# Second layer's latents taken from the un-normalised stream: a change to a two-block transformer kernel

## The chip, the cores and the metric

The kernel runs on one core of one Trainium2 chip. The metric is the device time of one execution in microseconds (us), of which the span from the first to the last instruction of the profile is nearly all.

## The reference, cut to what matters

A first block (two attention layers) is followed by a second block of two like layers. Each layer of the second block computes this on a stream `x` of 512 tokens by 1024 features in fp32:

```python
for l in range(2):
    h = rmsnorm(x, pre_norm_g[l])              # x * rsqrt(mean(x*x) + eps) * g
    proj = h @ w_in[l]
    (u, v, z_a, c_q, c_kv, k_rope, z_b, x_c, z_c, g_a, g_b, g_c) = jnp.split(proj, cuts, axis=-1)
    y_a = gmlp_spatial(u, v, ...) * silu(z_a)
    y_b = mla_attention(c_q, c_kv, k_rope, ...) * silu(z_b)
    y_c = rg_lru(x_c, ...) * silu(z_c)
    merged = sigmoid(g_a)*(y_a @ w_a) + sigmoid(g_b)*(y_b @ w_b) + sigmoid(g_c)*(y_c @ w_c)
    x = x + rmsnorm(merged @ w_out[l], post_norm_g[l])
```

`mla_attention` begins with `rmsnorm(c_q)` (384 wide, 3 tiles of 128) and `rmsnorm(c_kv)` (256 wide, 2 tiles); these five tiles are "the latents". `k_rope` is rotated by position and not normalised.

## The kernel before, in words

Features lie on the 128 partitions, the 512 tokens along the free axis, so `x` is 8 tiles of 128 x 512. A product in near-fp32 is three matmuls: every weight and every activation is split into an upper part (rounded) and a lower part (the rest), and upper*upper, upper*lower and lower*upper are added up in one bank (`products`, L553). One output tile of a 1024-wide input is thus 8 x 3 = 24 matmuls.

Weights come as a stream of slots of 128 x 1024 in an order written out by hand (`layer_stream`): in each layer of the second block ckv0, ckv1, cq0, cq1, cq2, kr, zb0, zb1, uv0, uv1, up0 and so on. SyncE's queue loads a slot into one of two raw buffers as soon as the slot two places before it has been split; ScalarE rounds it into one of five ring places (L1220) when TensorE has given that place back; GpSimd subtracts to get the lower part in four pieces (L507). ScalarE issues its rounding inside its own fixed order of work (`feed`, called from `next_job`), so a slot is rounded only when ScalarE comes to that point of its program. All five engines run such written-out programs and wait on semaphores.

The place of the change is the turn from layer 0 to layer 1 of the second block. TensorE ends layer 0 with the eight jobs of `wo`; ScalarE copies each into `mixed` and squares it; the squares are added up over the partitions by a matmul with ones into the bank `stat`; ScalarE takes logarithm and exponential of the sum (`root`), and VectorE turns that into the inverse root by four operations (`inverse`, L1713 to L1719). VectorE then walks the eight tiles: scale `mixed` (L1724), add it to `x` (L2226). Behind it ScalarE squares each new tile of `x` (L1257), and TensorE adds up all eight squares by eight matmuls with ones. After the second root VectorE makes the inverse root of the pre-norm and walks the eight tiles again in `norm_in`: `h` = x * gain * inverse root, split into upper and lower, three operations a tile (L1724, L1728, L1729). TensorE runs a `group` of four latents at once, tile by tile as `h` comes, then cq2, the sum of the squares of ckv (`latent_sum`), kr, zb0, the sum of the squares of cq, the rotation of kr, zb1, uv0 and uv1, and then the first job of `up`. VectorE adds up the latents' squares (L2079), makes two inverse roots and splits five tiles into `y` (the `c` tiles, ckv first), from which uv and up read; `up` needs all of them.

At the start of layer 0 the kernel already works in the other way: ckv0 is projected tile by tile from `unscaled`, which is x * gain without the inverse root, and ckv1, cq and kr follow from it too. The latents are normalised afterwards anyway, so the missing factor cancels (the epsilon is put back by L2076); kr is multiplied by the inverse root on VectorE (L2088). There `h` is made by VectorE while TensorE runs these six jobs, and zb0 is the first job that reads `h`.

Of the kernel before, what the change touches and what calls it, by code (L numbers as in the profile page):

```python
# [25 lines left out]
P = 128  # L26
# [172 lines left out]
def build(nc, stream, x_in, mem_in, pos_in, const_in, tables_in, first_in, layer_in, rows_in, ws_in, out, plans):  # L199
# [312 lines left out]
    def pe_program(pe):  # L512
# [37 lines left out]
        def mm(o, lhsT, rhs, start, stop):  # L550
            return nc.tensor.matmul(o, lhsT, rhs, start=start, stop=stop)  # L551
# [86 lines left out]

        def group(S, C, W, slots, src, key, joins=(0, 0, 0, 0)):

            j0 = C.n["job"]
            ahead = [b for b in range(len(slots)) if joins[b] == 0]

            def term(b, k, w, v, start=False, stop=False):
                return mm(token_bank(j0 + b, b)[:, :], W.slot(slots[b])(k * P, k * P + P)[w], src[:, k, v, :], start, stop)

            for b in ahead:
                W.need(slots[b])  # L650
                if b == 0:
                    pe.wait_ge(*S.after(*(("h_upper", *key(0)[1:-1]) if key(0)[0] == "h" else key(0))))
# [44 lines left out]

        def added_squares(S, C, tag):
# [6 lines left out]
            mm(stat[:, :], c("ones"), std[:, (m + 1) % 2, :], True, False)  # L705
# [262 lines left out]
        for l in range(LAYERS):  # L968
# [3 lines left out]
            if l == 0:  # L972
                w = W.slot("ckv0")
                for k, _ in enumerate(job_units(S, C, W, [("ckv0", w(k * P, k * P + P), both(unscaled, k, 0, SEQ),
                                                           ("unscaled", k)) for k in range(KT)])):
                    if k == 3:
                        added_squares(first, C, "b")
                W.finish("ckv0")
                for name in ["ckv1"] + names("cq", QR) + ["kr"]:
                    full(S, C, W, name, unscaled, None)  # L980
                latent_sum("ckv", raw[:, 1, :])
            else:
                group(S, C, W, names("ckv", KVR) + names("cq", QR)[:2], h, hkey)
                full(S, C, W, "cq2", h, hkey)
                latent_sum("ckv", raw[:, 1, :])
# [206 lines left out]
            if l < LAYERS - 1:  # L1192
                squares(S, C, c("ones"), KT)
                continue
# [8 lines left out]
    def act_program(act):  # L1203
# [32 lines left out]

        def unscaled_upper(k):

            nc.scalar.activation(unscaled[:, k, 0, :], x[:, k, :], ACT.Copy, scale=lc(0, "pre", k))\
                .then_inc(*layers[0].mark("upper_rounded", ("unscaled_upper", k)))  # L1240

# [189 lines left out]
        for l, s in enumerate("ab"):  # L1431
# [73 lines left out]
            if s == "a":  # L1505
# [3 lines left out]
                    between=lambda i: memory_key(0) if s == "a" and i == 6 else None,  # L1509
                    behind=lambda i: unscaled_upper(i) if s == "b" else None)  # L1510
        act.dma_start(rot[:, :, :], tables_in).then_inc(cols_loaded, 16)

        for l in range(LAYERS):
# [16 lines left out]

            if l:
                root(S, C, 1.0 / (P * KVR), alone=True)
            if l:
                take_head()
            else:
                next_job(S, C)
                C.next("head")
            if l == 0:
                root(S, C, 1.0 / (P * KVR), alone=True, eps=False)
                take(S, C, b_gate(0), keys_=[("b_raw", 0)])  # L1540
            root(S, C, 1.0 / (P * QR), alone=True, eps=l > 0)
            if l == 0:
                loaded[0] = None
                act.wait_ge(*S.after("b_raw", 0))
                nc.scalar.activation(b_gate(0), b_gate(0), ACT.Silu).then_inc(*S.mark("taken", ("silu", "b", 0)))
            for t in range(1 if l == 0 else 0, 2):
                take(S, C, b_gate(t), ACT.Silu, keys_=[("silu", "b", t)])
            for g in range(2):
# [146 lines left out]
    def dve_program(dve):  # L1695
# [64 lines left out]

        def unscaled_lower(k):

            S = layers[0]
            dve.wait_ge(*S.after("unscaled_upper", k))
            link(S, nc.vector.scalar_tensor_tensor(out=unscaled[:, k, 1, :], in0=x[:, k, :], scalar=lc(0, "pre", k),
                                                   in1=unscaled[:, k, 0, :].bitcast(FP32), op0=ALU.mult, op1=ALU.subtract),
                 ("unscaled", k))
# [9 lines left out]

        def add_square(S, m, tag, i):

# [3 lines left out]
            dve.wait_ge(*S.after("sq", t))  # L1783
            acc = std[:, (m + 1) % 2, :]
            link(S, nc.vector.tensor_tensor(acc, sq[:, (t - 1) % 2, :] if i == 1 else acc, sq[:, t % 2, :], ALU.add),
# [169 lines left out]
        for l, s in enumerate("ab"):  # L1955
# [89 lines left out]
            for k in range(KT):  # L2045
# [12 lines left out]
                if s == "b" and k:  # L2058
                    unscaled_lower(k - 1)
        unscaled_lower(KT - 1)  # L2060
        inv = next_norm(S, C)

        for l in range(LAYERS):
            S = layers[l]
            norm_in(S, C, h, x, lambda k: lc(l, "pre", k), (), inv, own=l > 0)
            dve.wait_ge(cols_loaded, 16 * (l + 1))
            C.n["job"] += QR + KVR

            def add_latent(tag, acc, a, n):


                for i in range(l, n):
                    dve.wait_ge(*S.after("latent_sq", a + i))
# [4 lines left out]
                    else:  # L2078
                        link(S, nc.vector.tensor_tensor(acc, latent_sq[:, a, :] if l and i == 1 else acc,  # L2079
                                                        latent_sq[:, a + i, :], ALU.add), *done)  # L2080

# [3 lines left out]
            j = C.next("job")  # L2085
            if l == 0:
                dve.wait_ge(*S.after("job", j))
                link(S, nc.vector.tensor_tensor(nrm[:, n % 2, :], proj[j % 2][:, :], inv[1], ALU.mult),  # L2088
                     ("nrm", n), ("read", j), ("std_used", inv[0]))
            for name, a, tiles in (("ckv", QR, KVR), ("cq", 0, QR)):  # L2090
                m, sd = inverse(S, C, alone=1.0 / (P * tiles), eps=EPS if l else 0.0)
                for k in range(a, a + tiles):
# [324 lines left out]
```

## Time and profile before

| | |
|---|---|
| median of 3 runs | 2281.86 us (2278.32 to 2282.83) |
| the profiled execution | 2283.95 us, of which its span is 2282.1 us |
| mean granted TensorE clock | 0.987 of full speed |

A row of a timeline has the start in us, the duration in us, the engine, the line, the operation and the tiles; in square brackets the idle time before it and what ended that. PE is TensorE, DVE VectorE, ACT ScalarE, POOL GpSimd. Matmuls overlap, so their durations add up to more than the time that they take; starts are the better measure.

### The profile page before, as it was taken

What the parts mean: (1) busy time and instruction counts of PE and PEld (TensorE: products, weight loads), DVE (VectorE), ACT (ScalarE), POOL (GpSimd) and SP (SyncE); (2) the same over time, 40 slices, a digit from 0 to 9 for tenths busy, and PEclk for the clock granted to TensorE, in tenths of its full rate; (3) what the DMA queues carried; (4) which work ended last, traced back from release to release, by engine and by line L of the source; (5) the groups of instructions that cost most, each with busy time, mean ns of one, the idle gap of its engine ahead of it and who ended that gap; (6) DMA issues with size and microseconds to landing.
All of it is one profiled execution on the core that took longest, in us unless ns stands there. A gap on an engine that the chain in (4) does not pass through costs nothing.

```text
span 2282.1 us, 27440 instructions
## 1 busy us (share of the span) xinstructions
PE 2201.7 (96%) x10006; PEld 1695.3 (74%) x10006; DVE 1195.3 (52%) x1827; ACT 938.4 (41%) x1591; POOL 1157.0 (51%) x1360
## 2 busy tenths in 40 slices
PE   7999999999899999999999999799999999999998
PEld 5776567765587668888887788576678888877886
DVE  6877885558667341043248853564420342197642
ACT  4546643356444543232234622344532322237322
POOL 4553236642175224565466675263145665575852
PEclk9999999999999999999999999999999999999999
DMA  3222122321132113332233233122033332332321
GB/s 146 76 82 74 38 74 93 102 68 41 32 102 87 52 42 128 101 100 84 92 95 99 74 111 102 55 85 64 30 109 93 99 96 85 100 102 74 112 91 65
DMA packets 53127, 191.45 MB, mean 84 GB/s; under 512 B 6016, under 2 KB 6400, under 8 KB 52480
## 3 DMA queue, kind: packets, MB, share of 16 engines
q1 hardware_dynamic: 51696, 184.44, 25.7%
q10 hardware_dynamic: 1296, 5.24, 0.6%
q8 instruction: 81, 1.33, 0.2%
q14 instruction: 54, 0.44, 0.1%
HBM read 187.56 MB, written 2.10 MB: 83 GB/s over the span
## 4 chain that ended last, share of the span: by engine, by line
PE 80%; DVE 13%; ACT 3%; issue 2%; POOL 1%; DMA 1%; SPq 0%; DVEq 0%; ACTq 0%
PE proj L555 20%; PE proj L557 19%; PE proj L556 19%; PE score L551 4%; PE proj L551 3%; PE stat L551 2%; PE turned L551 2%; PE mix L551 2%; DVE small L1835 2%; PE score L555 2%; PE score L557 1%; PE score L556 1%; DVE tmp L1724 1%; PE ptp L802 1%; DVE prob L1824 1%
## 5 line engine op out<-in xcount | busy, mean ns | idle before, releaser
L507 POOL TENSOR_TENSOR lower<-raw_ring,upper 128x256 fp32r<-128x256 f32 x1340 | 1140.9, 884 | 1070.5 <-ACT upper L1220 1070.1
L555 PE MATMUL proj<-h,upper 128*128 128x512 f32 x1408 | 569.4, 404 | 9.3 <-DVE h L1729 2.7
L1220 ACT ACTIVATE upper<-raw_ring 128x1024 fp32r<-128x1024 f32 x335 | 351.6, 1060 | 543.4 <-PE proj L555 298.6
L557 PE MATMUL proj<-h,lower 128*128 128x512 f32 x1408 | 549.7, 390 | 0.0
L556 PE MATMUL proj<-h,upper 128*128 128x512 f32 x1408 | 549.1, 390 | 0.0
L555 PEld LDWEIGHTS proj<-h,upper 128*128 128x128 f32 x1408 | 265.0, 188 | 73.4 <-issue 5.9
L557 PEld LDWEIGHTS proj<-h,lower 128*128 128x128 f32 x1408 | 264.6, 188 | 56.4
L556 PEld LDWEIGHTS proj<-h,upper 128*128 128x128 f32 x1408 | 265.3, 188 | 50.4 <-issue 1.9
L555 PE MATMUL proj<-y,upper 128*128 128x512 f32 x586 | 234.8, 401 | 8.2 <-ACT qk L1324 5.7
L556 PE MATMUL proj<-y,upper 128*128 128x512 f32 x586 | 230.0, 393 | 0.0
L557 PE MATMUL proj<-y,lower 128*128 128x512 f32 x586 | 229.8, 392 | 0.0
L555 PEld LDWEIGHTS proj<-y,upper 128*128 128x128 f32 x586 | 111.1, 190 | 39.7 <-ACT qk L1324 7.1
L557 PEld LDWEIGHTS proj<-y,lower 128*128 128x128 f32 x586 | 111.1, 190 | 23.7
L556 PEld LDWEIGHTS proj<-y,upper 128*128 128x128 f32 x586 | 111.2, 190 | 22.9 <-issue 1.0
L2127 DVE TENSOR_TENSOR merged<-proj,gate 128x512 f32<-128x512 f32 x16 | 11.1, 692 | 154.2 <-PE proj L557 154.2
L1324 ACT ACTIVATE gate<-proj 128x512 f32<-128x512 f32 x48 | 28.8, 600 | 143.8 <-PE proj L557 143.8
L2130 DVE TENSOR_TENSOR tmp<-proj,gate 128x512 f32<-128x512 f32 x16 | 11.1, 692 | 140.3 <-PE proj L557 140.3
L802 PE MATMUL ptp<-const,prob 128*128 128x128 f32 x320 | 59.1, 281 | 9.5 <-DVE prob L1849 3.7
L1729 DVE TENSOR_TENSOR y<-tmp,y 128x512 fp32r<-128x512 f32 x62 | 64.1, 1033 | 2.1
L2182 DVE SCALAR_TENSOR_TENSOR tmp<-xpad,lcol,tmp 128x512 f32<-128x512 f32 x60 | 59.2, 986 | 2.1
L2160 DVE TENSOR_TENSOR tmp<-score,bs 128x512 f32<-128x512 f32 x16 | 11.1, 692 | 92.8 <-PE score L551 92.7
L1824 DVE TENSOR_TENSOR_SCAN prob<-prob 128x128 f32<-128x128 f32 (+3 forms) x48 | 44.5, 926 | 28.1 <-ACT prob L1348 26.7
(463 smaller groups left out, 3529.6 us busy)
## 6 DMA issues: line engine op xcount, KB each, us to landing
raw_ring<-stream SPq DMA_DIRECT2D x335, 512.0 KB, 3.5
landing<-stream SPq DMA_DIRECT2D x5, 512.0 KB, 9.3
x<-x_in SPq DMA_DIRECT2D x4, 512.0 KB, 6.0
rows<-rows_in ACTq DMA_DIRECT2D x2, 1024.0 KB, 5.3
out<-x SPq DMA_DIRECT2D x8, 256.0 KB, 2.4
memraw<-mem_in SPq DMA_DIRECT2D x1, 1024.0 KB, 12.6
memraw<-mem_in ACTq DMA_DIRECT2D x1, 1024.0 KB, 4.9
rot<-tables_in ACTq DMA_DIRECT2D x2, 512.0 KB, 4.0
```

Of the source, the lines that this page charges most:

```text
L507: ins = nc.gpsimd.tensor_tensor(lower[:, p % RING, a:b], slot_source(p)[:, a:b], upper[:, p % RING, a:b].bitcast(FP32), ALU.subtract)
L551: return nc.tensor.matmul(o, lhsT, rhs, start=start, stop=stop)
L555: first_ = nc.tensor.matmul(o, lhsT[0], rhs[0], start=start, stop=False)
L556: nc.tensor.matmul(o, lhsT[0], rhs[1], start=False, stop=False)
L557: return first_, nc.tensor.matmul(o, lhsT[1], rhs[0], start=False, stop=stop)
L802: ins = nc.tensor.transpose(bank_[:, kb * P:kb * P + P], src[:, kb * P:kb * P + P], c("ident"))
L1220: nc.scalar.activation(upper[:, p % RING, :], slot_source(p), ACT.Copy).then_inc(split_upper, 1)
L1324: nc.scalar.activation(dst, src[:, 0:cols], func, **more)\
L1729: link(S, nc.vector.tensor_tensor(dst[:, 1, :], src, dst[:, 0, :].bitcast(FP32), ALU.subtract), *keys_)
L1824: link(S, nc.vector.tensor_tensor_scan(rest[:, 0:n][:, ::-1], rest[:, 0:n][:, ::-1], rest[:, 0:n][:, ::-1], 1.0, ALU.mult, ALU.min))
L1835: link(S, nc.vector.reduce_max(small[:, 24 + b % 4:25 + b % 4], scores4[b % 4][:, 0:keys(kind, i)], AX_X))
L2182: link(S, nc.vector.scalar_tensor_tensor(out=dst, in0=src[:, k:k + SEQ], scalar=lc(l, "conv", LT * k + t), in1=dst, op0=ALU.mult, op1=ALU. ...
```

## The change

For layer 1 the kernel does what layer 0 does, with these differences: the update of `x` and the un-normalised split go together on VectorE (scale, add to `x`, add a square, lower part), four latents are projected at once (`group`), and the squares of `x` 0 to 5 are added up on VectorE into `raw[:, 1, :]`, so that TensorE adds three operands by ones in place of eight. That sum stands in TensorE's program in front of the group's last tile. ScalarE rounds the upper part (`unscaled_upper`) behind each square. The order after the group is that of layer 0: cq2, kr, sum of ckv, zb0, sum of cq. The diff, cut to its core:

```diff
-    unscaled = place("unscaled", at_y + 8 * 2 * SEQ, [P, KT, 2, SEQ], FP32R)
+    unscaled = [place(f"unscaled{l}", at, [P, KT, 2, SEQ], FP32R) for l, at in enumerate((at_y + 8 * 2 * SEQ, at_y + 13 * SEQ))]
...
             for k in range(1, KT):                       # in group(..., before_last=lambda: None)
+                if k == KT - 1:
+                    before_last()
                 pe.wait_ge(*S.after(*key(k)))
...
             else:                                        # TensorE, layer 1
-                group(S, C, W, names("ckv", KVR) + names("cq", QR)[:2], h, hkey)
-                full(S, C, W, "cq2", h, hkey)
-                latent_sum("ckv", raw[:, 1, :])
-                full(S, C, W, "kr", h, None)
-            full(S, C, W, "zb0", h, None if l else hkey)
+                group(S, C, W, names("ckv", KVR) + names("cq", QR)[:2], unscaled[1], lambda k: ("unscaled", k),
+                      before_last=lambda: added_squares(layers[0], C, "pre", raw[:, 1, :]))
+                for name in ("cq2", "kr"):
+                    full(S, C, W, name, unscaled[1], None)
+            latent_sum("ckv", raw[:, 1, :])
+            full(S, C, W, "zb0", h, hkey)
...
             added_squares(S, C, "wo")                    # TensorE, end of layer 0
             if l < LAYERS - 1:
-                squares(S, C, c("ones"), KT)
                 continue
...
             if l < LAYERS - 1:                           # ScalarE, end of layer 0
-                squares(S, C, [(x[:, k, :], ("x", k)) for k in range(KT)], 1.0 / DM)
+                plans["squares_at", (l, "pre")] = C.n["sq"]
+                squares(S, C, [(x[:, k, :], ("x", k)) for k in range(KT)], 1.0 / DM, behind=lambda i: unscaled_upper(1, i))
                 continue
...
                 step(S, nc.vector.tensor_tensor(x[:, d, :], x[:, d, :], mixed[:, d, :], ALU.add), ("x", d), ("std_used", m))
+                if l < LAYERS - 1 and d:                 # VectorE, end of layer 0
+                    add_square(S, m + 1, "pre", d - 1, raw[:, 1, :])
+                    unscaled_lower(1, d - 1)
             if l < LAYERS - 1:
+                unscaled_lower(1, KT - 1)
                 inv = next_norm(S, C)
```

`add_square` does something for tiles 1 to 5 alone. The rest of the diff makes the branches of layer 0 hold for both layers: the epsilon goes into VectorE's sum of the latents' squares (one operation more for each of ckv and cq), kr is scaled on VectorE, zb0's gate is copied first and put through Silu behind the second root.

## Rows read from the trace of the kernel before

**Rows 1.** The page: the chain that ended last, by engine.
```profile
PE 80%; DVE 13%; ACT 3%; issue 2%; POOL 1%; DMA 1%; SPq 0%; DVEq 0%; ACTq 0%
```

**Rows 2.** Stretches: PE, PEld, DVE, ACT, POOL busy; granted clock, DMA share, GB/s.
```profile
1452.00:1474.00 22.00, 10.73 (x16) 3.61 (x16) 17.74 (x25) 8.91 (x13) 0.00 (x0) 0.84 0.00 0
1474.00:1480.00 6.00, 5.80 (x19) 4.50 (x20) 5.76 (x8) 1.06 (x1) 3.80 (x4) 0.72 0.00 0
...
692.00:694.00 2.00, 0.61 (x3) 0.23 (x2) 1.93 (x3) 0.00 (x0) 1.11 (x1) 1.00 0.00 0
```

**Rows 3.** Timeline of all engines at the turn to layer 1.
```profile
1439.67 0.69 DVE L1785 TENSOR_TENSOR std<-std,sq 128x512 f32<-128x512 f32 x1 [4.75 <-ACT sq L1685]
...
1455.64 0.75 DVE L1724 SCALAR_TENSOR_TENSOR mixed<-mixed,lcol,std 128x512 f32<-128x512 f32 x1
...
1467.01 0.69 DVE L2226 TENSOR_TENSOR x<-x,mixed 128x512 f32<-128x512 f32 x1
...
1470.44 0.69 DVE L1713 TENSOR_SCALAR gate<-stat 128x512 f32<-128x512 f32 x1 [2.73 <-ACT std L1277]
...
1474.20 0.76 PE L551 MATMUL proj<-h,upper 128*128 128x512 f32 x1 [4.59 <-issue]
```

**Rows 4.** Timeline of VectorE in layer 1, from the normalised tiles on.
```profile
1473.34 0.75 DVE L1724 SCALAR_TENSOR_TENSOR h<-x,lcol,std 128x512 fp32r<-128x512 f32 x1
...
1490.35 0.69 DVE L1729 TENSOR_TENSOR h<-tmp,h 128x512 fp32r<-128x512 f32 x1
1499.00 0.96 DVE L2079 TENSOR_TENSOR raw<-latent_sq 128x512 f32<-128x512 f32 x1 [7.95 <-ACT latent_sq L1523]
...
1510.51 0.69 DVE L1713 TENSOR_SCALAR half_var<-stat 128x512 f32<-128x512 f32 x1
...
1532.67 1.11 DVE L1729 TENSOR_TENSOR y<-craw,y 128x512 fp32r<-128x512 f32 x1
```

**Rows 5.** Timeline of TensorE in layer 1: first matmuls of cq2, zb0 and up.
```profile
1497.70 0.39 PE L555 MATMUL proj<-h,upper 128*128 128x512 f32 x1
...
1509.62 0.50 PE L555 MATMUL proj<-h,upper 128*128 128x512 f32 x1
...
1533.83 0.50 PE L555 MATMUL proj<-y,upper 128*128 128x512 f32 x1 [0.31 <-DVE y L1729]
```

**Rows 6.** The chain that ended last, in order of time: six matmuls of the group.
```profile
1482.90 1.36 PE score L551 x6
```

**Rows 7.** Tile `unscaled`: operations, min/median/max ns, first and last start.
```profile
L1239 ACT ACTIVATE unscaled<-x,lcol x8: 709/711/717, 635.1 to 658.8; 128x512 fp32r<-128x512 f32 x8
L1765 DVE SCALAR_TENSOR_TENSOR unscaled<-x,lcol,unscaled x8: 754/1107/1112, 636.0 to 659.6; 128x512 fp32r<-128x512 f32 x8
```

**Rows 8.** Timeline of VectorE at the start of layer 0.
```profile
663.30 0.69 DVE L1713 TENSOR_SCALAR gate<-stat 128x512 f32<-128x512 f32 x1 [2.96 <-ACT std L1277]
...
666.21 0.75 DVE L1724 SCALAR_TENSOR_TENSOR h<-x,lcol,std 128x512 fp32r<-128x512 f32 x1
...
690.27 1.11 DVE L1729 TENSOR_TENSOR h<-tmp,h 128x512 fp32r<-128x512 f32 x1
...
692.56 1.09 DVE L2079 TENSOR_TENSOR raw<-raw,latent_sq 128x512 f32<-128x512 f32 x1
...
696.59 0.69 DVE L1713 TENSOR_SCALAR half_var<-stat 128x512 f32<-128x512 f32 x1
...
716.29 1.11 DVE L1729 TENSOR_TENSOR y<-craw,y 128x512 fp32r<-128x512 f32 x1
```

**Rows 9.** Timeline of TensorE at the start of layer 0: sums, and up's first matmul.
```profile
659.74 1.02 PE L551 MATMUL stat<-std,const 128*128 128x512 f32 x2
...
693.80 1.10 PE L551 MATMUL stat<-raw,const 128*128 128x512 f32 x2 [1.39 <-DVE raw L2079]
...
718.29 0.39 PE L555 MATMUL proj<-y,upper 128*128 128x512 f32 x1
```

**Rows 10.** Timeline of GpSimd at the start of layer 0.
```profile
666.32 8.73 POOL L507 TENSOR_TENSOR lower<-raw_ring,upper 128x256 fp32r<-128x256 f32 x8 [3.01 <-ACT upper L1220]
```

More of the change, by code:

```diff
@@ L637, in tokens, with group @@
                 W.finish(name)
-        def group(S, C, W, slots, src, key, joins=(0, 0, 0, 0)):
+        def group(S, C, W, slots, src, key, joins=(0, 0, 0, 0), before_last=lambda: None):
             j0 = C.n["job"]
@@ L651, in group @@
                 if b == 0:
-                    pe.wait_ge(*S.after(*(("h_upper", *key(0)[1:-1]) if key(0)[0] == "h" else key(0))))
+                    first_key = {"h": ("h_upper", *key(0)[1:-1]), "unscaled": ("unscaled_upper", 0)}
+                    pe.wait_ge(*S.after(*first_key.get(key(0)[0], key(0))))
                 hold(S, j0 + b, b)
@@ L696, in squares, with added_squares @@
                 ins.then_inc(*S.mark("summed", ("sq_used", t), ("sums", m)))
-        def added_squares(S, C, tag):
+        def added_squares(S, C, tag, acc=None):
             m = C.next("norm")
@@ L704, in added_squares @@
             pe.wait_ge(*S.after("added", tag))
-            mm(stat[:, :], c("ones"), std[:, (m + 1) % 2, :], True, False)
+            mm(stat[:, :], c("ones"), std[:, (m + 1) % 2, :] if acc is None else acc, True, False)
             for i in (t - 1, t):
@@ L973, in pe_program @@
                 w = W.slot("ckv0")
-                for k, _ in enumerate(job_units(S, C, W, [("ckv0", w(k * P, k * P + P), both(unscaled, k, 0, SEQ),
+                for k, _ in enumerate(job_units(S, C, W, [("ckv0", w(k * P, k * P + P), both(unscaled[0], k, 0, SEQ),
                                                            ("unscaled", k)) for k in range(KT)])):
@@ L979, in pe_program @@
                 for name in ["ckv1"] + names("cq", QR) + ["kr"]:
-                    full(S, C, W, name, unscaled, None)
-                latent_sum("ckv", raw[:, 1, :])
-            else:
-                group(S, C, W, names("ckv", KVR) + names("cq", QR)[:2], h, hkey)
-                full(S, C, W, "cq2", h, hkey)
-                latent_sum("ckv", raw[:, 1, :])
-                full(S, C, W, "kr", h, None)
-            full(S, C, W, "zb0", h, None if l else hkey)
+                    full(S, C, W, name, unscaled[0], None)
+            else:
+                group(S, C, W, names("ckv", KVR) + names("cq", QR)[:2], unscaled[1], lambda k: ("unscaled", k),
[4 more added lines that the diff above has]
+            full(S, C, W, "zb0", h, hkey)
             latent_sum("cq", raw[:, 0, :])
@@ L1235, in feed_one, with unscaled_upper @@
             feed(min(fed[0] + 1, wanted[0]))
-        def unscaled_upper(k):
-            nc.scalar.activation(unscaled[:, k, 0, :], x[:, k, :], ACT.Copy, scale=lc(0, "pre", k))\
-                .then_inc(*layers[0].mark("upper_rounded", ("unscaled_upper", k)))
+        def unscaled_upper(l, k):
+            nc.scalar.activation(unscaled[l][:, k, 0, :], x[:, k, :], ACT.Copy, scale=lc(l, "pre", k))\
+                .then_inc(*layers[l].mark("upper_rounded", ("unscaled_upper", k)))
         def squares(S, C, srcs, scale, cols=SEQ, jobs=False, tag=None, between=lambda i: None, behind=lambda i: None):
@@ L1509, in act_program @@
                     between=lambda i: memory_key(0) if s == "a" and i == 6 else None,
-                    behind=lambda i: unscaled_upper(i) if s == "b" else None)
+                    behind=lambda i: unscaled_upper(0, i) if s == "b" else None)
         act.dma_start(rot[:, :, :], tables_in).then_inc(cols_loaded, 16)
@@ L1529, in take_head @@
                 take(S, C, nrm[:, k % 2, :], keys_=[("nrm", k)], waits=[("nrm_used", k - 2)] if k >= head0 + 2 else [])
[L1531 to L1547, printed above, removed]
+            next_job(S, C)
+            C.next("head")
+            root(S, C, 1.0 / (P * KVR), alone=True, eps=False)
+            take(S, C, b_gate(0), keys_=[("b_raw", 0)])
+            root(S, C, 1.0 / (P * QR), alone=True, eps=False)
+            loaded[0] = None
+            act.wait_ge(*S.after("b_raw", 0))
+            nc.scalar.activation(b_gate(0), b_gate(0), ACT.Silu).then_inc(*S.mark("taken", ("silu", "b", 0)))
+            take(S, C, b_gate(1), ACT.Silu, keys_=[("silu", "b", 1)])
             for g in range(2):
@@ L1759, in next_norm, with unscaled_lower @@
             return inverse(S, C, alone=1.0 / DM, minus_half=gate[:, 1, :])
-        def unscaled_lower(k):
-            S = layers[0]
+        def unscaled_lower(l, k):
+            S = layers[l]
             dve.wait_ge(*S.after("unscaled_upper", k))
-            link(S, nc.vector.scalar_tensor_tensor(out=unscaled[:, k, 1, :], in0=x[:, k, :], scalar=lc(0, "pre", k),
-                                                   in1=unscaled[:, k, 0, :].bitcast(FP32), op0=ALU.mult, op1=ALU.subtract),
+            link(S, nc.vector.scalar_tensor_tensor(out=unscaled[l][:, k, 1, :], in0=x[:, k, :], scalar=lc(l, "pre", k),
+                                                   in1=unscaled[l][:, k, 0, :].bitcast(FP32), op0=ALU.mult, op1=ALU.subtract),
                  ("unscaled", k))
@@ L1776, in rotate, with add_square @@
             step(S, nc.vector.tensor_tensor(dst, t, tmp[:, :], ALU.add), ("nrm_used", n), *keys_)
-        def add_square(S, m, tag, i):
+        def add_square(S, m, tag, i, into=None):
             if not 1 <= i < KT - 2:
@@ L1783, in add_square @@
             dve.wait_ge(*S.after("sq", t))
-            acc = std[:, (m + 1) % 2, :]
+            acc = std[:, (m + 1) % 2, :] if into is None else into
             link(S, nc.vector.tensor_tensor(acc, sq[:, (t - 1) % 2, :] if i == 1 else acc, sq[:, t % 2, :], ALU.add),
@@ L2058, in dve_program @@
                 if s == "b" and k:
-                    unscaled_lower(k - 1)
-        unscaled_lower(KT - 1)
+                    unscaled_lower(0, k - 1)
+        unscaled_lower(0, KT - 1)
         inv = next_norm(S, C)
@@ L2064, in dve_program @@
             S = layers[l]
-            norm_in(S, C, h, x, lambda k: lc(l, "pre", k), (), inv, own=l > 0)
+            norm_in(S, C, h, x, lambda k: lc(l, "pre", k), (), inv)
             dve.wait_ge(cols_loaded, 16 * (l + 1))
@@ L2069, in add_latent @@
             def add_latent(tag, acc, a, n):
-                for i in range(l, n):
+                for i in range(n):
                     dve.wait_ge(*S.after("latent_sq", a + i))
@@ L2078, in add_latent @@
                     else:
-                        link(S, nc.vector.tensor_tensor(acc, latent_sq[:, a, :] if l and i == 1 else acc,
-                                                        latent_sq[:, a + i, :], ALU.add), *done)
+                        link(S, nc.vector.tensor_tensor(acc, acc, latent_sq[:, a + i, :], ALU.add), *done)
             add_latent("ckv", raw[:, 1, :], 0, KVR)
@@ L2085, in dve_program @@
             j = C.next("job")
[L2086 to L2089, printed above, removed]
+            dve.wait_ge(*S.after("job", j))
+            link(S, nc.vector.tensor_tensor(nrm[:, n % 2, :], proj[j % 2][:, :], inv[1], ALU.mult),
+                 ("nrm", n), ("read", j), ("std_used", inv[0]))
             for name, a, tiles in (("ckv", QR, KVR), ("cq", 0, QR)):
-                m, sd = inverse(S, C, alone=1.0 / (P * tiles), eps=EPS if l else 0.0)
+                m, sd = inverse(S, C, alone=1.0 / (P * tiles), eps=0.0)
                 for k in range(a, a + tiles):
```

## The prediction

> **What bounds the kernel now.** I read the page first: TensorE makes 80% of the chain that ended last, VectorE 13% [rows 1]. So time is to be won only where TensorE stands still, and the change touches one such place, the turn from layer 0 to layer 1. The stretches show it: from 1452 to 1474 TensorE has 10.7 us of work in 22, all of it sums of squares, and GpSimd has none [rows 2]. The timeline says what TensorE waits for. VectorE updates the eight tiles of x from 1455.64 to 1467.70, the sum follows, the pre-norm's first operation starts at 1470.44, and the group of four latents starts at 1474.20 [rows 3]. That is the stall that the change aims at.
>
> What comes behind it matters as much. VectorE makes h until 1491.04, then waits 8 us and more for the latents' squares, and from 1510.51 it works without a pause to 1533.78 [rows 4]. TensorE's first `up` matmul, at 1533.83, waits 0.31 us for VectorE's last c tile [rows 5]. So at the end of this stage VectorE and TensorE arrive together: VectorE is a second chain, as long as TensorE's. From `up` on the two programs are the same, so the whole question is when `up` starts, and every us there is a us of the total.
>
> The start of layer 0 is the same program as layer 1 after the change, from the pre-norm's sum on. There VectorE's pre-norm starts at 663.30 [rows 8] and `up` at 718.29 [rows 9].
>
> **The change part by part.**
>
> *The loop over x.* Before, a tile costs VectorE a scale and an add, eight tiles 12.06 us [rows 3]. Five additions of squares come in; the nearest row is 0.69 us, 0.73 with the gap to the next start [rows 3], together 3.65. Eight lower parts come in. Their rows go from 0.754 to 1.11 us [rows 7]; the low end is with GpSimd idle. GpSimd is idle here too (22 us of zero), and stays so, because ScalarE's next rounding stands behind the root in its program. I take 0.754, 0.79 with the gap; the high end would add 7 x 0.35 = 2.5 us. Seven of them lie in front of the group's tile 6: 5.53. Tile 6 is ready at 1455.64 + 12.06 + 3.65 + 5.53 = 1476.9. ScalarE's eight added roundings hide behind VectorE's 3.03 us a tile; uncovered they would cost 0.71 each [rows 7].
>
> *The sum.* It now stands in TensorE's program behind tile 6. Twelve matmuls take 2.72 us at the group's pace [rows 6]. TensorE keeps pace with 3.03 us a tile, but starts cold and reaches tile 6 some 0.4 us late (estimate: the first tile's twelve at half pace take 5.1 us, and 0.3 a tile is made good): 1477.3 + 2.7 = 1480.0. From the first of the three sum matmuls to the norm's first operation is 663.30 - 659.74 = 3.56 us in layer 0 [rows 8, 9]. The norm thus starts at 1483.6, where it was at 1470.44: **13.2 us later**. The five sum matmuls saved ran inside VectorE's loop and give nothing.
>
> *From the norm to `up`.* Before: 1533.83 - 1470.44 = 63.4 us [rows 3, 5]. Layer 0 does it in 718.29 - 663.30 = 55.0 us [rows 8, 9]: **8.4 us less**. I take layer 0's value, since the order is the same: norm_in takes 690.27 + 1.11 - 666.21 = 25.2 us there [rows 8], the sum of ckv is ready at 693.65, `up` follows 24.5 us after the sum's matmul at 693.80, and the last c tile is ready at 717.40, 0.9 before `up`. In layer 1 before, norm_in took only 17.7 us [rows 4]. The difference is GpSimd: in layer 0 it begins to split slots 0.1 us after norm_in begins [rows 10], and VectorE's operations stretch (the last of a tile 0.69 against 1.11) [rows 4, 8]. After the change ScalarE comes to the rounding of cq2 behind the root and the table load, as it does in layer 0 with kr, so GpSimd starts at about 1486.5, together with norm_in, and has six slots to do there: cq2, kr, zb0, zb1, uv0, uv1. I take 25.2; the low end is 17.7.
>
> *What TensorE does in between.* The group ends behind the sum's three matmuls (some 2.6 of the 3.56 us) and tile 7's twelve, at about 1485.3. cq2's lower part comes only at about 1490.8 (GpSimd start plus half of the 8.73 us of two slots [rows 10]), so a first new wait of 5 us stands there; cq2 and kr (24 matmuls each, 5.4 us at the group's pace [rows 6]) end at 1502. Then `latent_sum` waits for VectorE, whose norm_in ends at 1486.5 + 25.2 = 1511.7, plus 2.3 for two additions: 1514. A second new wait, 12 us. In layer 0 this wait was 1.4 us [rows 9], because the norm there came early under a job that still had most of its matmuls ahead. The 22 us of idle time are not removed but moved behind the group.
>
> *The clock.* After the short wait of layer 0 TensorE goes on at full speed, 1.00 in that stretch; after the idle 4.6 us in front of the group it runs at a mean of 0.72 over 6 us, that is partly at 1.2 GHz [rows 2, 3]. The 12 us wait is more like the second. Price: 0.28 x 5.8 = **1.6 us**, bounds 0 and 1.6. The Trainium skill (TensorE: Matmul & The Clock Gate, "Why this matters for your kernels") speaks against such gaps: idle time between bursts drops the clock to half. By that rule the 1.6 us are lost for sure, and the sum is as below; if the clock held as behind layer 0's short wait, the sum would be 1.6 lower.
>
> *The rest* (epsilon, kr on VectorE, zb0's gate copied first, ScalarE's two table loads) is in layer 0's 55.0 us already.
>
> **Sum:** 13.2 - 8.4 + 1.6 = +6.4 us. Against the profiled execution, 2283.95 + 6.4 = 2290.3. That execution lies 2.09 above the median of the runs, so 2288.2 for the median, 0.28% more. The forecast's own range is 2286 to 2291: without the clock's price +4.8, with the dear lower parts +8.9; VectorE's second half, 23.3 us in layer 1 against 20.8 in layer 0 [rows 4, 8], is nearly covered by the 0.9 us and the clock's 1.6.
>
> **The rivals.**
>
> *GpSimd does not stretch norm_in.* Not slower. If norm_in takes 17.7 us as in layer 1 before [rows 4], and the two additions 1.5, the sum's matmul is at 1483.6 + 2.9 + 17.7 + 1.6 = 1505.8 and `up` at 1530.3: -3.5 us, 2278.4, within 0.2%. It decides below about 21 us of norm_in, where the sum is back at zero (+6.4 less the clock's 1.6 less 4.4). For it: layer 1's last tiles ran unstretched (0.69 for the last operation) [rows 4]. Against: GpSimd was idle then, and will not be. The Trainium skill (GPSIMD Engine Reference, "Specifications") has the two engines contend for their SBUF interfaces when VectorE reads two SBUF tensors; by it norm_in stretches whenever GpSimd runs, and the stretched row of layer 0 agrees. 15%; a mixture in between, +1 to +4.5 us, gets another 16%.
>
> *TensorE's early start is kept.* If VectorE could feed it without waits, `up` would start 35 us of matmuls and sums (1533.83 - 1497.70 less the waits, 36.1 - 0.8) [rows 5] after the group's end at 1485.3, at 1520.6: -13 us, 2269. It needs h by 1496, 10 us after the norm's inverse root, and eight tiles have no row under 17.7. 6%, with all that ends over 0.2% faster.
>
> *The group runs cold.* If the waits between tiles keep TensorE at 1.2 GHz, a tile takes 12 x 0.45 = 5.4 us (twice the time of [rows 6]) in place of 3.03, and the norm starts some 15 us later still: 2303. Against: TensorE is busy nine tenths of each tile. 4%.
>
> **How the numbers follow.** Forecast 59%, the rivals as given. 0.2% is 4.6 us, about what a measurement of this kernel can tell from no change. Faster by more: 6%. Slower by more: forecast without its low edge, 55%, and the cold group, 4%, so 59%. Within: 35%. The 8-in-10 range reaches from under the unstretched norm_in (2278) to the forecast's upper end (2291.5), which leaves out the early start, the cold group and a few per cent at either end.
>
> **What would show it.** In the profile after: x's last addition near 1476, the norm's first operation near 1483.6, GpSimd's first slot beside norm_in's first tile, norm_in of about 25 us, a wait of TensorE in front of cq2 for GpSimd and one of about 12 us in front of the sum of ckv for VectorE, `up` at about 1540. I am wrong if norm_in stays near 18 us, if the norm starts before 1480, or if `up` starts before 1534.

## The result, and the profile after

| | before | after |
|---|---|---|
| median of the timed runs | 2281.6 us (2276.5 to 2285.6, 10 runs) | 2286.7 us (2285.0 to 2290.4, 10 runs) |
| span of the profiled execution | 2282.1 us | 2285.7 us |
| ratio of the runs, 95% interval | | 1.0026 (1.0018 to 1.0034) |

The change costs 5.1 us by the medians. The forecast was 2288.2, slower by more than 0.2%; the interval's lower end, 0.18%, lies just under that bound.

To compare executions I use one stretch, called the stage: from VectorE's first scale of the loop over x to the first matmul of `up` [rows 3, 5]. Before it lasts 1533.83 - 1455.64 = 78.2 us, after 1537.68 - 1452.03 = 85.65, so 7.5 us more. Behind `up` nothing moved (748.3 us to the end of the span before, 748.0 after). Ahead of it the profiled execution of after came 3.6 us earlier to the same point, though the change touches nothing there; that is why the two spans differ by only 3.6. This is scatter: in the profiles below, which share that part, the first scale comes anywhere from 1451.68 to 1455.79.

TensorE's share of the chain that ended last fell from 80% [rows 1] to 78%, as the page of after shows:

```profile
PE 78%; DVE 13%; ACT 4%; issue 2%; POOL 1%; DMA 1%; SPq 0%; DVEq 0%; ACTq 0%
```

The timeline of VectorE in after: first scale, a lower part, the last add to x, the norm's first operation, the first h operation, one steady tile of h, the last h operation, the second addition for ckv, the first operation of ckv's inverse root, two operations of the second c tile, the last c tile.

```profile
1452.03 0.75 DVE L1719 SCALAR_TENSOR_TENSOR mixed<-mixed,lcol,std 128x512 f32<-128x512 f32 x1
...
1455.06 0.75 DVE L1760 SCALAR_TENSOR_TENSOR unscaled<-x,lcol,unscaled 128x512 fp32r<-128x512 f32 x1
...
1471.78 0.69 DVE L2219 TENSOR_TENSOR x<-x,mixed 128x512 f32<-128x512 f32 x1
...
1480.19 0.69 DVE L1708 TENSOR_SCALAR gate<-stat 128x512 f32<-128x512 f32 x1 [5.53 <-ACT std L1279]
...
1483.09 0.75 DVE L1719 SCALAR_TENSOR_TENSOR h<-x,lcol,std 128x512 fp32r<-128x512 f32 x1
...
1486.14 1.10 DVE L1719 SCALAR_TENSOR_TENSOR tmp<-x,lcol,std 128x512 f32<-128x512 f32 x1
1487.28 0.83 DVE L1723 CAST h<-tmp 128x512 fp32r<-128x512 f32 x1
1488.14 1.10 DVE L1724 TENSOR_TENSOR h<-tmp,h 128x512 fp32r<-128x512 f32 x1
...
1506.73 1.09 DVE L1724 TENSOR_TENSOR h<-tmp,h 128x512 fp32r<-128x512 f32 x1
...
1508.99 1.09 DVE L2074 TENSOR_TENSOR raw<-raw,latent_sq 128x512 f32<-128x512 f32 x1
...
1513.02 0.69 DVE L1708 TENSOR_SCALAR half_var<-stat 128x512 f32<-128x512 f32 x1
...
1519.51 0.75 DVE L1719 SCALAR_TENSOR_TENSOR craw<-craw,lcol,std 128x512 f32<-128x512 f32 x1
1520.29 0.43 DVE L1723 CAST y<-craw 128x512 fp32r<-128x512 f32 x1
...
1532.57 1.10 DVE L1724 TENSOR_TENSOR y<-craw,y 128x512 fp32r<-128x512 f32 x1
```

The norm's first operation is 28.2 us behind the first scale, where it was 14.8 [rows 3]; h takes 24.7 us (1483.09 to 1507.82) in place of 17.7 [rows 4]. GpSimd's timeline in after shows what runs beside h: it begins with h's first tile.

```profile
1483.20 8.65 POOL L507 TENSOR_TENSOR lower<-raw_ring,upper 128x256 fp32r<-128x256 f32 x8 [37.95 <-ACT upper L1222]
1492.34 3.91 POOL L507 TENSOR_TENSOR lower<-raw_ring,upper 128x256 fp32r<-128x256 f32 x4 [0.49 <-ACT upper L1222]
...
1514.59 4.33 POOL L507 TENSOR_TENSOR lower<-raw_ring,upper 128x256 fp32r<-128x256 f32 x4 [5.06 <-ACT upper L1222]
1524.88 8.24 POOL L507 TENSOR_TENSOR lower<-raw_ring,upper 128x256 fp32r<-128x256 f32 x8 [5.96 <-ACT upper L1222]
```

From 1518.92 to 1524.88 GpSimd stands still, and there VectorE's scale takes 0.75 us and its rounding 0.43, where beside GpSimd's work in h they take 1.10 and 0.83.

TensorE's timeline in after: the sum of the squares of x, cq2's first matmul, the sum of ckv, two of the matmuls of zb0 that follow it, the first matmul of `up`. (A matmul with ones stands as two in the profile.)

```profile
1476.62 1.02 PE L551 MATMUL stat<-raw,const 128*128 128x512 f32 x2
...
1487.97 0.77 PE L555 MATMUL proj<-unscaled,upper 128*128 128x512 f32 x1 [5.86 <-POOL lower L507]
...
1510.23 2.04 PE L551 MATMUL stat<-raw,const 128*128 128x512 f32 x2 [8.99 <-DVE raw L2074]
...
1512.50 0.63 PE L556 MATMUL proj<-h,upper 128*128 128x512 f32 x1
1512.93 0.63 PE L557 MATMUL proj<-h,lower 128*128 128x512 f32 x1
...
1537.68 0.39 PE L555 MATMUL proj<-y,upper 128*128 128x512 f32 x1
```

The 22 us stretch of sums [rows 2] is gone, and two waits stand in its place: 5.9 us for GpSimd in front of cq2, 9.0 us for VectorE in front of the sum of ckv. Behind the second, matmuls follow each other every 0.43 us instead of 0.23. The stretches of after show the clock behind each wait (columns as in [rows 2]): 0.50 is the 1.2 GHz level. Behind the wait in front of cq2 it is back at 2.4 GHz from about 1492, behind the second from about 1516.

```profile
1488.00:1492.00 4.00, 4.00 (x10) 3.13 (x11) 3.86 (x5) 0.80 (x1) 3.85 (x4) 0.50 0.41 131
...
1510.00:1516.00 6.00, 5.77 (x12) 3.89 (x13) 5.73 (x9) 2.17 (x3) 1.41 (x2) 0.50 0.27 87
1516.00:1522.00 6.00, 6.00 (x23) 4.23 (x22) 5.76 (x8) 1.89 (x4) 2.92 (x3) 0.97 0.28 90
```

### The profile page after: what moved, and what is told of

It is laid out like the page before. It is cut to its first block, busy times and chain, and to the rows that moved or that the text cites. A ratio compares the mean times of both kernels' runs of the same rounds, so it can differ in the third digit from the quotient of the medians.

```text
span 2285.7 us, 27460 instructions
## 1 busy us (share of the span) xinstructions
PE 2194.2 (96%) x9996; PEld 1692.6 (74%) x9996; DVE 1211.0 (53%) x1843; ACT 941.0 (41%) x1599; POOL 1162.6 (51%) x1360
## 4 chain that ended last, share of the span: by engine, by line
PE 78%; DVE 13%; ACT 4%; issue 2%; POOL 1%; DMA 1%; SPq 0%; DVEq 0%; ACTq 0%
PE proj L555 20%; PE proj L557 19%; PE proj L556 19%; PE score L551 4%; PE proj L551 3%; PE stat L551 3%; PE turned L551 2%; DVE small L1830 2%; PE mix L551 2%; DVE tmp L1719 1%; POOL lower L507 1%; PE score L555 1%; PE score L557 1%; PE score L556 1%; DVE h L1724 1%
## 5 line engine op out<-in xcount | busy, mean ns | idle before, releaser
L557 PE MATMUL proj<-h,lower 128*128 128x512 f32 x1392 | 544.2, 391 | 0.0
L2120 DVE TENSOR_TENSOR merged<-proj,gate 128x512 f32<-128x512 f32 x16 | 11.1, 692 | 154.2 <-PE proj L557 154.2
L2123 DVE TENSOR_TENSOR tmp<-proj,gate 128x512 f32<-128x512 f32 x16 | 11.1, 692 | 140.3 <-PE proj L557 140.3
L2153 DVE TENSOR_TENSOR tmp<-score,bs 128x512 f32<-128x512 f32 x16 | 11.1, 692 | 92.8 <-PE score L551 92.8
L1819 DVE TENSOR_TENSOR_SCAN prob<-prob 128x128 f32<-128x128 f32 (+3 forms) x48 | 44.4, 926 | 28.1 <-ACT prob L1350 26.7
```

The source lines that it names most:

```text
L557: return first_, nc.tensor.matmul(o, lhsT[1], rhs[0], start=False, stop=stop)
L1819: link(S, nc.vector.tensor_tensor_scan(rest[:, 0:n][:, ::-1], rest[:, 0:n][:, ::-1], rest[:, 0:n][:, ::-1], 1.0, ALU.mult, ALU.min))
```

## The experiments

Theory: VectorE's one chain, x loop, norm, h, sums for ckv, c tiles, sets the start of `up`, and the change made that chain longer. Rivals: TensorE's waits for GpSimd's lower parts, or the clock, are the cause. The profile of after already narrows the theory: the last c tile is ready at 1533.67, 4.0 us before `up`, and from the sum of ckv on TensorE waits for nothing. So in after VectorE's chain can set no more than the sum of ckv; the 27.45 us from there to `up` are TensorE's own work. All edits are to the changed kernel. Each ratio is of medians, from 3 or 5 rounds (10 to 12 runs) beside the kernel before on the same chip.

| kernel | first scale at | norm behind first scale | h takes | wait for ckv | stage | ratio to before (95%) |
|---|---|---|---|---|---|---|
| before | 1455.64 | 14.8 | 17.7 | - | 78.2 | 1 |
| after | 1452.03 | 28.2 | 24.7 | 9.0 | 85.65 | 1.0026 (1.0018 to 1.0034) |
| sum_two_tiles_earlier | 1454.37 | 23.2 | 24.75 | 11.1 | 79.8 | 1.0008 (0.9998 to 1.0017) |
| cq2_rounded_early | 1451.68 | 28.1 | 23.9 | 14.2 | 83.8 | 1.0018 (1.0008 to 1.0027) |
| lower_parts_left_out | 1451.75 | 28.1 | 16.1 | 5.5 | 74.9 | 0.9979 (0.9970 to 0.9989) |
| ckv_added_inside | 1454.58 | 28.1 | 27.65 | 0 | 84.3 | 1.0017 (1.0007 to 1.0026) |
| kept_warm | 1452.87 | 28.15 | 24.9 | filled | 82.8 | 1.0014 (1.0005 to 1.0023) |
| squares_on_tensor | 1453.05 | 22.4 | 20.05 | 0 | 78.8 | 1.0000 (0.9991 to 1.0008) |
| squares_on_tensor_ckv_inside | 1455.79 | 23.1 | 23.8 | 0 | 79.3 | 1.0002 (0.9993 to 1.0010) |
| h_rounded_on_scalar | 1452.34 | 28.15 | 18.6 | 3.05 | 78.7 | 0.9990 (0.9981 to 0.9999) |
| h_rounded_on_scalar_sum_early | 1453.71 | 23.2 | 18.7 | 5.0 | 73.95 | 0.9981 (0.9972 to 0.9989) |

(us; each from the kernel's own timeline. "h takes" in the two kernels with ckv inside holds those additions too.) The stage is that of one execution, the ratio that of the runs; as differences to before the two agree within 3 us.

**The sum two tiles earlier.** In after the sum starts at 1476.62, but all three operands are ready at 1473.19: VectorE adds the last of its six squares at 1469.47, and ScalarE's square of the last tile is this row.

```profile
1472.56 0.63 ACT L1259 ACTIVATE sq<-x 128x512 f32<-128x512 f32 x1 [1.78 <-DVE x L2219]
```

Only the place in TensorE's program makes the sum wait.

```diff
-                if k == KT - 1:
+                if k == KT - 3:
                     before_last()
```

> The sum of the squares of x stands in TensorE's program in front of the group's tile 5 in place of tile 7; nothing else is changed. The stage is measured from VectorE's first scale of the loop over x to the first matmul of up: 78.2 us before, 85.65 after the change. If VectorE's chain from the pre-norm on decides (theory), the norm's first operation comes at 23 us of the stage in place of 28.2, bound by the last square alone, and up comes as much earlier: a stage of 80 to 81.5. If TensorE's own work and its wait for cq2 decide (rival), the group ends no earlier and the stage stays at 85 to 86.

The norm starts 5.0 us earlier, 23.2 us behind the first scale, as VectorE's timeline of this kernel shows, with TensorE's first matmul of `up`:

```profile
1477.54 0.69 DVE L1708 TENSOR_SCALAR gate<-stat 128x512 f32<-128x512 f32 x1 [0.54 <-ACT std L1279]
```

```profile
1534.14 0.39 PE L555 MATMUL proj<-y,upper 128*128 128x512 f32 x1
```

The stage is 5.9 us shorter, just under the 80 to 81.5 expected, and the whole no longer differs from before by what the runs can tell. cq2's wait falls to 0.5 as well, since GpSimd starts earlier, while the wait for ckv grows from 9.0 to 11.1: TensorE has the same matmuls in between and is sooner through.

**cq2 rounded ahead of the root.** ScalarE rounds cq2 behind the last square, before logarithm and table load.

```diff
-..., behind=lambda i: unscaled_upper(1, i))
+..., behind=lambda i: (unscaled_upper(1, i), i == KT - 1 and feed(fed[0] + 1)))
```

> ScalarE rounds the slot of cq2 right behind the last tile of x, ahead of the root and the table load, so that GpSimd splits it while VectorE waits for the sum. Both theories expect TensorE's 5.9 us wait in front of cq2 to go. If that wait is only a part of a longer one behind kr (theory: VectorE decides), the wait in front of the sum of ckv grows by nearly as much and the stage falls by less than 2 us from 85.65, by what norm_in gains from one slot less beside it. If every idle us of TensorE counts (rival), the stage falls by 5 to 6 us to about 80.

TensorE's timeline of this kernel, cq2 and the sum of ckv, and VectorE's second addition for ckv:

```profile
1482.80 0.50 PE L555 MATMUL proj<-unscaled,upper 128*128 128x512 f32 x1 [1.10 <-ACT latent_sq L1525]
...
1508.18 2.05 PE L551 MATMUL stat<-raw,const 128*128 128x512 f32 x2 [14.19 <-DVE raw L2074]
```

```profile
1507.35 0.69 DVE L2074 TENSOR_TENSOR raw<-raw,latent_sq 128x512 f32<-128x512 f32 x1
```

The wait in front of cq2 falls from 5.9 to 1.1, and the wait for ckv grows from 9.0 to 14.2. Of 4.8 us taken away TensorE hands 5.2 to the next wait. That `up` still starts 1.8 us earlier goes with VectorE: h is 0.8 us shorter with one slot less for GpSimd to do beside it, and the two additions for ckv take 0.69 us each in place of 1.09, another 0.8, since GpSimd has ended its slots at 1505.58. The lower parts' lateness is not what sets `up`.

**The lower parts left out.** GpSimd subtracts only the last 16 columns of ten slots, so it hardly runs beside h.

```diff
-            for a in range(0, SLOT, SLOT // 4):
-                b = a + SLOT // 4
+            left_out = NF + NL + 4 <= p < NF + NL + 14
+            for a, b in [(SLOT - 16, SLOT)] if left_out else [(n * SLOT // 4, (n + 1) * SLOT // 4) for n in range(4)]:
```

> GpSimd leaves out all but the last 16 of the 1024 columns of the lower weight parts of ten slots of layer 1 (cq2 to up3), so those products are made with old lower parts; order and waits stay. If GpSimd's work stretches VectorE's operations (theory), norm_in falls from 24.7 us to 16 to 17.7, the last c tile comes 12 to 15 us earlier, and the stage falls by 9 to 12 us to 74 to 77, then bound by TensorE's order behind the sum of ckv. If VectorE is slow for another reason (rival), norm_in stays at 24 to 25 us and only the wait for cq2 shrinks: a stage of 84.5 to 86.

VectorE's timeline of this kernel, one tile of h from its rounding on and the last operation, and TensorE's first matmul of `up`:

```profile
1487.82 0.43 DVE L1723 CAST h<-tmp 128x512 fp32r<-128x512 f32 x1
1488.28 0.69 DVE L1724 TENSOR_TENSOR h<-tmp,h 128x512 fp32r<-128x512 f32 x1
...
1498.18 0.69 DVE L1724 TENSOR_TENSOR h<-tmp,h 128x512 fp32r<-128x512 f32 x1
```

```profile
1526.64 0.39 PE L555 MATMUL proj<-y,upper 128*128 128x512 f32 x1
```

The rounding takes 0.43 against 0.83 in after, the subtraction 0.69 against 1.10. h takes 16.1 us, the c tiles come sooner as well, and the stage is 10.8 us shorter. This is the prediction's rival "GpSimd does not stretch norm_in" brought about by force: it gave -3.5 us against before, and the stage is 3.3 us under before's. But this edit takes away two things, the contention and TensorE's waits for lower parts; a later experiment separates them. The Trainium skill (SBUF — State Buffer, "Who interferes with whom") says that VectorE's copies and casts can contend with GpSimd, when their operands allow a mode with two ports, and that an instruction with two inputs in SBUF contends with a GpSimd instruction that reads SBUF. The trace agrees in kind: all three operations of a tile stretch in after. No run here shows how the two engines take turns.

**ckv's squares added inside h.** VectorE adds them behind tile 4 instead of tile 7.

```diff
-            norm_in(S, C, h, x, lambda k: lc(l, "pre", k), (), inv)
...
-            add_latent("ckv", raw[:, 1, :], 0, KVR)
+            norm_in(S, C, h, x, lambda k: lc(l, "pre", k), (), inv,
+                    aside=lambda k: l and k == 4 and add_latent("ckv", raw[:, 1, :], 0, KVR))
...
```

> In layer 1 VectorE adds up the squares of ckv behind tile 4 of norm_in in place of behind tile 7, so that TensorE's sum of ckv does not wait for the end of norm_in and zb0 is made tile by tile. If what follows is then bound by VectorE's last c tile (theory), up comes with it, at 81.5 to 82.5 us of the stage in place of 85.65, and the 9 us wait in front of the sum falls below 2 us, with zb0 drawn out in its place. If zb0 behind the last tile of h decides anyway (rival), the stage stays within 1 us of 85.65.

TensorE's timeline of this kernel: the sum of ckv, two matmuls of zb0, the sum of cq and `up`; then VectorE's last c tile.

```profile
1504.07 1.02 PE L551 MATMUL stat<-raw,const 128*128 128x512 f32 x2
...
1510.05 0.50 PE L555 MATMUL proj<-h,upper 128*128 128x512 f32 x1 [0.83 <-DVE h L1724]
...
1513.30 0.79 PE L555 MATMUL proj<-h,upper 128*128 128x512 f32 x1 [2.28 <-DVE h L1724]
...
1518.15 2.07 PE L551 MATMUL stat<-raw,const 128*128 128x512 f32 x2 [3.21 <-DVE half_var L1708]
...
1538.87 0.39 PE L555 MATMUL proj<-y,upper 128*128 128x512 f32 x1
```

```profile
1535.23 0.69 DVE L1724 TENSOR_TENSOR y<-craw,y 128x512 fp32r<-128x512 f32 x1
```

The 9.0 us wait is gone entirely, and only 1.4 us of the stage with it: more than the rival allowed, less than the theory asked for. TensorE now waits inside zb0 for tiles of h, then for VectorE to read ckv's sum out of the bank `stat`, so the same VectorE chain releases it, one job later. The sum of cq comes 4.0 us earlier in the stage than in after (63.6 against 67.6), but from there to `up` it takes 20.7 us against 18.1, since the matmuls behind these waits begin at half speed (granted clock 0.50 from 1516 to 1522). `up` is not bound by the last c tile here, as the theory had it: that is ready at 1535.92, 2.95 us before `up`.

**Kept warm.** Ten matmuls with ones into a bank that nobody reads stand where TensorE waits for ckv.

```diff
+                for _ in range(10):
+                    mm(ptp[:, :], c("ones"), x[:, 0, :], True, True)
             latent_sum("ckv", raw[:, 1, :])
```

> Ten matmuls of ones by a tile of x into a bank that nothing reads (0.86 us each, 8.6 in all) fill most of TensorE's 9 us wait in front of the sum of ckv; nothing else is changed. The prediction priced the clock that falls in this wait at 1.6 us; in the profile after, the sum's matmul to up's first takes 27.4 us, where layer 0 takes 24.5. If the clock is the difference (theory), it falls to about 24.5 and the stage from 85.65 to 82.5 to 83. If it is something else (rival: the last c tile, or a bank), it stays near 27.

In the stretch behind the sum the granted clock of this kernel is 1.00, where after has 0.50:

```profile
1511.00:1517.00 6.00, 6.00 (x25) 4.52 (x25) 5.76 (x8) 2.19 (x3) 2.40 (x3) 1.00 0.33 90
```

and from the sum to `up` its timeline has 24.5 us, layer 0's value, against 27.45 in after:

```profile
1511.17 1.10 PE L551 MATMUL stat<-raw,const 128*128 128x512 f32 x2
...
1535.68 0.45 PE L555 MATMUL proj<-y,upper 128*128 128x512 f32 x1
```

So the clock costs 2.9 us of the stage here, and the sum of ckv stays where it was in the stage (58.3 us against 58.2). The Trainium skill (TensorE: Matmul & The Clock Gate, "Why this matters for your kernels") says that idle time between bursts drops the clock to half; the trace agrees, 9 us of idle and then 0.50. VectorE's last c tile is now ready at 1535.58, 0.1 us ahead of `up`, so more speed on TensorE would bring nothing.

**The squares back on TensorE.** VectorE's additions of squares are dropped, and the eight squares are added up on TensorE inside the group, 0 to 2 in front of tile 1, 3 to 7 in front of tile 2.

```diff
-                    add_square(S, m + 1, "pre", d - 1, raw[:, 1, :])
...
-                if k == KT - 1:
-                    before_last()
+                before(k)      # {1: sums_of_x(0, 3), 2: sums_of_x(3, KT)}
```

> The squares of x are added up by TensorE again, eight matmuls with ones, as in the kernel before, but all of them put ahead of the group's tiles 2 to 7 (three behind tile 0, five behind tile 1); VectorE's five additions go. The projection from the un-normalised tiles stays. If the pre-norm's start decides (theory), VectorE's loop takes 2.3 us a tile, the norm's first operation comes at 19 to 21 us of the stage (28.2 after the change, 14.8 before), and the stage is 74 to 78, at or under the 78.2 of before, though the group ends at 35 us in place of 30. If TensorE's later group decides (rival), the stage is 85 us or more.

The norm's first operation comes 22.4 us behind the first scale, later than the 19 to 21 expected: the squares wait in ScalarE for their two buffers, and TensorE, delayed in front of them, does the last sum at half clock (1.95 us). The stage is 6.8 us shorter than after's and 0.65 longer than before's; 74 to 78 was expected. Not all of the gain is the norm's: h takes 20.05 us in place of 24.7, because GpSimd stands still from 1483.1 to 1491.8, in the middle of it, and the rounding takes 0.43 us there and 0.85 before and after. TensorE's timeline of this kernel shows what ends last:

```profile
1505.63 0.50 PE L555 MATMUL proj<-h,upper 128*128 128x512 f32 x1 [2.15 <-ACT latent_sq L1534]
...
1531.89 0.50 PE L555 MATMUL proj<-y,upper 128*128 128x512 f32 x1 [0.83 <-DVE y L1733]
```

The group now ends later, so the latents' squares come later, and VectorE waits 2.7 us for them where TensorE had waited for VectorE.

**Two edits for VectorE together.** The squares on TensorE and ckv's additions inside h.

> The kernel before this one and the squares of ckv added inside norm_in, behind its tile 4. If VectorE's chain from the norm's first operation to the last c tile (53 us) is then all that is left (theory), up comes at 72 to 75 us of the stage, 3 to 6 us under the 78.2 of before, and the whole is 0.1 to 0.3% faster than before. If TensorE, whose group and latents now end later (46 us), becomes the bound (rival), the stage is that of the run without this step, within 1 us.

The stage is 79.3 us, no shorter than with the squares alone: the rival was right here. Inside h, VectorE waits 1.2 us for ckv's squares, and `up` still waits 1.9 us for the last c tile. An addition moved ahead does not shorten a chain that has to do it anyway.

**Rounding on ScalarE.** GpSimd keeps its whole work, and for tiles 1 to 7 one operation in three leaves VectorE's h.

```diff
+    h_scaled = lambda k: raw[:, 0, :] if k % 2 else tmp[:, :]
...
+                for i in ((1,), (2, 3), (4, 5), (6, 7), ())[n] if l else ():     # ScalarE, behind latent n
+                    act.wait_ge(*S.after("h_scaled", i))
+                    nc.scalar.activation(h[:, i, 0, :], h_scaled(i), ACT.Copy)\
+                        .then_inc(*S.mark("upper_rounded", ("h_rounded", i)))
...
+                    link(S, scaled(h_scaled(k), x[:, k, :], lc(l, "pre", k), inv[1]), ("h_scaled", k))
+                    # then, one tile behind: wait for ("h_rounded", k - 1), subtract
```

> The changed kernel, but for tiles 1 to 7 of layer 1's normalised tiles VectorE makes only the scaled tile and the lower part, and ScalarE rounds the upper part (0.71 us a tile, in the gaps between its latents); the scaled tile goes by turns into two buffers. GpSimd's work stays as it is. Seven operations of 0.83 us leave VectorE. Theory (VectorE's chain from the norm to the sum of ckv sets the start of up, with GpSimd's stretch in it): the tiles take about 19 us (3.1 for the first, 14 operations of 1.11 and their gaps) in place of 24.7, the wait in front of the sum of ckv falls from 9.0 to about 3.5 us, and up starts 5 to 8 us earlier: a stage of 78 to 80.5 in place of 85.65, the whole within 0.2% of the kernel before, ratio 0.998 to 1.001. Rival (with fewer lower parts up came earlier because TensorE no longer waited for GpSimd): cq2's wait of 5.9 us stays and the stage stays above 84, ratio about 1.002. Second rival: ScalarE comes late with a rounded tile and the tiles take over 22 us.

TensorE's timeline of this kernel: cq2, the sum of ckv, two matmuls of zb0, `up`.

```profile
1488.27 0.76 PE L556 MATMUL proj<-unscaled,upper 128*128 128x512 f32 x1 [5.86 <-POOL lower L508]
...
1504.41 1.10 PE L552 MATMUL stat<-raw,const 128*128 128x512 f32 x2 [3.05 <-DVE raw L2091]
...
1505.58 0.40 PE L557 MATMUL proj<-h,upper 128*128 128x512 f32 x1
1505.82 0.40 PE L558 MATMUL proj<-h,lower 128*128 128x512 f32 x1
...
1531.05 0.50 PE L556 MATMUL proj<-y,upper 128*128 128x512 f32 x1 [1.96 <-DVE y L1729]
```

The wait for GpSimd is what it was, 5.86 us, and yet the stage is 6.9 us shorter. This settles the question that leaving out the lower parts had left open: it is VectorE's time, not TensorE's wait for the lower parts. Of the 6.9 us 6.1 lie ahead of the sum of ckv (52.1 us behind the first scale, 58.2 in after). With only 3.05 us of idle the matmuls behind the sum go on at 0.23 us.

**With the sum early too.** The same and the first experiment's edit.

> The same, and the sum of the squares of x stands two tiles earlier in TensorE's program, in front of tile 5 of the group. Theory: the two savings add up, since they lie one behind the other on VectorE's chain (5 us ahead of the norm, 5 to 6 behind it): the norm's first operation 23.2 us after the first scale, the tiles about 19 us, the sum of ckv some 47 us after the first scale with a wait of about 5 us, up at a stage of 72 to 75 where the kernel before has 78.2: faster than the kernel before by 3 to 6 us, ratio 0.9975 to 0.9987. Rival: with VectorE 10 us earlier TensorE's own matmuls, or the latents' squares and ScalarE's order, set the start of up, and the stage stays at 77 or above, as with the squares on TensorE.

VectorE's norm and TensorE's sum of ckv and `up` in this kernel's timelines:

```profile
1476.87 0.69 DVE L1713 TENSOR_SCALAR gate<-stat 128x512 f32<-128x512 f32 x1 [0.54 <-ACT std L1280]
```

```profile
1500.87 2.04 PE L552 MATMUL stat<-raw,const 128*128 128x512 f32 x2 [5.02 <-DVE raw L2091]
...
1527.66 0.40 PE L556 MATMUL proj<-y,upper 128*128 128x512 f32 x1
```

Both savings arrive: the stage is 73.95 us, 11.7 under after's and 4.2 under before's. The runs give 2277.2 against 2282.3 us, ratio 0.9981 (0.9972 to 0.9989). The interval lies under 1 and under the change's own (1.0018 to 1.0034): this version beats both kernels. So the un-normalised stream pays here once VectorE's chain is shortened by as much as the change had lengthened it. Whether the kernel before would gain from rounding on ScalarE too was not run.

## Why the prediction was right, and where it was off

- **The norm, 13.2 us later.** Measured 28.16 - 14.80 = 13.4. VectorE's loop has the predicted 3.03 us a tile, with the lower parts at 0.75 us, the low end chosen because GpSimd is idle (37.95 us of idle in its row). Taking the sum two tiles forward shows that 5.0 of the 13.4 us come from its place in TensorE's program; the other 8.4 are what the loop on VectorE now does (last addition to x 19.75 us behind the first scale, 11.37 before).
- **From the norm to `up`, layer 0's 55.0 us.** Measured 57.5. Up to the sum of ckv it is 30.0 us against layer 0's 30.5 (h 24.7 against 25.2 predicted). From there to `up` it is 27.45 against 24.5: the clock. As forecast, the last c tile is no longer what `up` waits for.
- **The clock, 1.6 us.** This is the mis-sized term. It was taken from the group's start before [rows 2], behind 4.6 us of idle; behind 9 us of idle half speed lasted some 6 us of matmuls, and keeping TensorE busy brought 2.9 us back. The forecast's own formula with the row of after, 0.50 x 5.77, gives 2.9. The bounds 0 and 1.6 were too narrow.
- **The sum.** 13.4 - 63.4 + 57.5 = +7.5 for the stage, forecast +6.4. The medians of the runs differ by 5.1, with an interval of 4.1 to 7.8 (0.0018 and 0.0034 of 2281.6).
- **The waits.** cq2 5.9 us for GpSimd (forecast 5), ckv 9.0 for VectorE (forecast 12). The second is shorter mainly because cq2, too, began at half speed behind its wait (0.50 from 1488 to 1492), which took TensorE some 2 us that it would else have waited. The forecast's "22 us of idle time" is the length of the stretch; TensorE was busy for 10.7 of it [rows 2], so 11.3 us of idle became 14.9 in two waits. Neither wait is a term of its own: with cq2's gone the next wait took it over, with ckv's gone other waits and the clock took all but 1.4 us.
- **GpSimd does not stretch norm_in** fell: 24.7 us with GpSimd at work, 16.1 without. The size that it would have had was right. "GpSimd was idle then" holds for layer 1's last tiles before, not for all: it worked 3.8 us beside the first ones [rows 2], which is in the 17.7. **The early start** fell: TensorE's waits show it. **The cold group** fell: the norm came when forecast, and from 1455 to 1476 the mean granted clock was 0.92.

## What to carry to other kernels

An engine that stands idle in a trace is not always the one to give work: here TensorE's 11 us of idle in a stretch of 22 were the shadow of VectorE's chain, and a change that filled them while putting thirteen operations more on VectorE ahead of a norm only moved the idle time behind the group. Price such a change on the chain that releases the next common point, and look up which point that is in each kernel (before, the c tiles for `up`; after, the sum of ckv, with 27.45 us of TensorE's own work behind it). Ask which engine with slack could take an operation from it; ScalarE had it. In a program whose order is written out, a reduction whose result others wait for belongs at the first place where its operands are ready: two tiles of matmuls in front of it cost 5 us here.

## What the runs showed of the hardware

A rounding copy on VectorE, one tensor in and one out, is stretched by GpSimd's subtraction as much as the operations with two tensors: 0.43 to 0.83 us, against 0.69 to 1.10 and 0.75 to 1.10. I had expected it of the two-input forms alone. And waits in front of a sum did not all have the same price: behind 3.05 us of idle zb0 ran at full speed, behind 5.02 and 8.99 us it began at half. The single wait does not tell it all: with ckv's additions inside h TensorE went on at half behind 3.21 us, where shorter waits had gone before.
